# Gates and branch projections of the later layers with tokens on the partitions, the gates' bias added by VectorE

## The reference

```python
h = rmsnorm(x, norm1_g[l])
u = h @ w_in[l]                              # q, k, v, glu_in, four_in
att = ...differential attention of q, k, v, 8 heads, normed
y_a = att @ w_proj_a[l]                      # 512 -> 1024
cv = layernorm(conv31(glu(glu_in)) + conv_b[l], ...)
y_b = jax.nn.silu(cv) @ w_proj_b[l]          # 512 -> 1024
y_c = real(fft2(four_in)) @ w_proj_c[l]      # 512 -> 1024
gates = jax.nn.sigmoid(h @ w_gate[l] + b_gate[l]).reshape(b, s, 3, d)
merged = gates[:, :, 0] * y_a + gates[:, :, 1] * y_b + gates[:, :, 2] * y_c
x = x + merged @ w_out[l]
...then a feed-forward block
```

## Time and profile before

| | us |
|---|---|
| three runs, median (lowest, highest) | 1252.49 (1251.73, 1252.96) |
| the profiled execution | 1253.01 |
| its span | 1251.7 |
| TensorE busy | 1245.6 |
| DVE busy | 948.0 |
| ACT busy | 716.4 |
| POOL busy | 438.8 |

### The profile page before, as it was taken

One profiled execution on the slowest core, in us unless ns is written; L12 is line 12 of the kernel. 1 busy time (PEld: TensorE's weight loads), 2 busy tenths in 40 slices (PEclk: granted clock), 3 DMA queues, 4 the chain that ended last, 5 costly groups with the idle time before them and its releaser, 6 DMA issues.

```text
span 1251.7 us, 18713 instructions
## 1 busy us (share of the span) xinstructions
PE 1245.6 (100%) x7472; PEld 1104.0 (88%) x7472; DVE 948.0 (76%) x1366; ACT 716.4 (57%) x1030; POOL 438.8 (35%) x346
## 2 busy tenths in 40 slices
PE   9999999999999999999999999999999999999999
PEld 7888888888888889999998888888999998888887
DVE  6875668677887478986767888986898586888895
ACT  7755445377765365565846556546456674655552
POOL 0010012039892069467440112008766743011100
PEclk9999999999999999999999999999999999999999
DMA  9753334455545447643455454455753444555443
GB/s 353 254 212 140 135 118 166 171 188 198 189 182 201 169 169 257 210 155 135 169 200 184 175 198 155 182 218 188 265 188 146 156 169 168 196 178 200 151 165 121
DMA packets 36566, 230.73 MB, mean 184 GB/s; under 512 B 4480, under 2 KB 5120, under 8 KB 10496
## 3 DMA queue, kind: packets, MB, share of 16 engines
q1 hardware_dynamic: 36480, 229.55, 51.0%
HBM read 222.19 MB, written 1.05 MB: 178 GB/s over the span
## 4 chain that ended last, share of the span: by engine, by line
PE 97%; DVE 1%; DMA 1%; ACT 1%; SPq 0%; issue 0%; DVEq 0%; ACTq 0%
PE ps L620 19%; PE ps L531 13%; PE ps L533 13%; PE ps L532 13%; PE ps L625 10%; PE ps L586 7%; PE ps L588 7%; PE ps L587 7%; PE ps L536 6%; PE ps L550 2%; DMA raw<-in_w 1%; PE ps L1174 1%; SPq L436 0%; PE ps L851 0%; DVE wlo L1994 0%; ACT whi L1260 0%
## 5 line engine op out<-in xcount | busy, mean ns | idle before, releaser
L1260 ACT ACTIVATE whi<-raw 128x2048 fp32r<-128x2048 f32 (+1 forms) x213 | 401.7, 1891 | 113.2 <-PE ps L533 83.9
L1994 DVE TENSOR_TENSOR wlo<-raw,whi 128x2048 fp32r<-128x2048 f32 (+2 forms) x169 | 383.2, 2273 | 90.1 <-ACT whi L1260 89.4
L1824 POOL TENSOR_TENSOR wlo<-raw,whi 128x512 fp32r<-128x512 f32 x176 | 226.7, 1320 | 90.5 <-ACT whi L1260 87.5
L620 PE MATMUL ps<-hh,whi 128*128 128x512 f32 x1056 | 255.8, 392 | 0.0
L620 PEld LDWEIGHTS ps<-hh,whi 128*128 128x128 f32 x1056 | 193.0, 188 | 36.5
L1796 POOL TENSOR_TENSOR st<-st,sm 128x1 f32<-128x1 f32 (+2 forms) x28 | 46.0, 1643 | 362.5 <-DVE st L2048 193.3
L586 PE MATMUL ps<-hh,whi 128*128 128x256 f32 x512 | 146.2, 285 | 0.0
L588 PE MATMUL ps<-hh,wlo 128*128 128x256 f32 x512 | 144.9, 283 | 0.0
L587 PE MATMUL ps<-hh,whi 128*128 128x256 f32 x512 | 144.8, 283 | 0.0
L625 PEld LDWEIGHTS ps<-hh,wlo 128*128 128x128 f32 x1056 | 137.8, 191 | 6.7
L625 PE MATMUL ps<-hh,wlo 128*128 128x256 f32 x1056 | 139.8, 283 | 0.0
(11 more groups left out here) (348 smaller groups left out, 2252.9 us busy)
## 6 DMA issues: line engine op xcount, KB each, us to landing
raw<-in_w SPq DMA_DIRECT2D x203, 1024.0 KB, 4.8
raw<-in_w SPq DMA_DIRECT2D x8, 256.0 KB, 7.0
kst<-kh SPq DMA_DIRECT2D x16, 128.0 KB, 2.6
qst<-qh SPq DMA_DIRECT2D x16, 128.0 KB, 2.4
raw<-in_w SPq DMA_DIRECT2D x2, 560.0 KB, 14.5
x<-in_x SPq DMA_DIRECT2D x2, 512.0 KB, 5.2
gain<-in_rows SPq DMA_DIRECT2D x2, 512.0 KB, 5.7
kst<-kl SPq DMA_DIRECT2D x8, 128.0 KB, 2.4
```

What stands on the lines that cost most here:

```text
L620: pe.op.matmul(o[:, :], wh[:, k, c], t.hh[:, k, :, :], start=k == 0, stop=False, skip_group_check=True)
L1260: act.op.activation(t.whi[i % NHI][:, c], t.raw[i % NRAW][:, c], ACT.Copy).then_inc(*at("act_hi", ("hi", i)))
L1824: pool.op.tensor_tensor(t.wlo[i % NRAW][:, half(k)], t.raw[i % NRAW][:, half(k)], t.whi[i % NHI][:, half(k)].bitcast(F32), ALU.subtract).t ...
L1994: dve.op.tensor_tensor(t.wlo[i % NRAW][:, c], t.raw[i % NRAW][:, c], t.whi[i % NHI][:, c].bitcast(F32), ALU.subtract).then_inc(*at("dve_lo ...
```

## The change

It is made in both later layers and in four parts.

- The gates and the projections pc, pa and pb are computed by `rows` and no more by `feats`. A gate unit is now 512 columns wide, 6 instead of 12 units per layer, in two chunks of 4 k each; a projection is one chunk as before. `rows_steps` learns units of one chunk. As a step of the back is now 6 matmuls of 512 columns, `weave` takes 2 for 4, and the other counts are about halved.
- The bias of a gate is a row now. SP loads 512 of its values, the same for all partitions, into one half of `gain`, two halves in turn, and DVE adds it as it evacuates the bank; ACT only takes sigmoids, of 128x1024 for a whole unit. Before it loads bias j (j from 2), SP waits for the additions of gate j - 2.
- DVE multiplies with the gate in halves of tokens, POOL adds the first two branches, and DVE adds the third. The mixed result is then turned by TensorE and split from PSUM, by the functions that the first layer uses; the first four turns stand in pb1 after two of its four steps.
- POOL raises two sums to powers before it splits the last chunk of pc, no more after it.

```diff
-        for f in GATES:
-            wide(f"g{l}_{f}", "w_gate_2", l, cols((256 * f, 256)), 8, 8)
+        for n in GATES:
+            wide(f"g{l}_{n}", "w_gate_2", l, cols((512 * n, 512)), 8, 4)
-GATES = (8, 9, 10, 11, 0, 1, 2, 3, 4, 5, 6, 7)
+GATES = (4, 5, 0, 1, 2, 3)
...
 def rows_steps(u):
-    c0, c1 = UNITS[u]
+    chunks = UNITS[u]
+    if len(chunks) == 2:
+        yield "take", chunks[0], 0, 0, 0
+        for k in range(4):
+            for tt in range(2):
+                yield "mul", chunks[0], k, k, tt
+            yield "step", chunks[0], 0, 0, 0
+    i = chunks[-1]
+    yield "take", i, 0, 0, 0
     for tt in range(2):
         for k in range(4):
-            yield "mul", c1, k, 4 + k, tt
+            yield "mul", i, k, 4 * len(chunks) - 4 + k, tt
...
+    def bias(l, j):
+        n = GATES[j]
+        load(f"d_bias{j % 2}", t.gain[:, half(j % 2)],
+             d["in_bias"][l:l + 1, 512 * n:512 * n + 512].to_broadcast([128, 512]), ("gate bias", l, n))
...
+            if i == UNITS[f"v{l}"][0]:
+                sp.wait_ge(*on("xn", ("n3", "n5")[l], 1, 1))
+                bias(l, 0)
+                bias(l, 1)
+            for j in range(2, 6):
+                if i == UNITS[f"g{l}_{GATES[j + 1]}" if j < 5 else f"pc{l}_0"][0]:
+                    sp.wait_ge(*on("gate biased", l, GATES[j - 2]))
+                    bias(l, j)
...
@@ pe_program @@
-            yield 9
+            yield 5
...
-            yield 7
+            yield 4
...
-        back = chain(*[feats(f"g{l}_{f}", *h, 8) for f in GATES],
-                     *[feats(f"pc{l}_{f}", t.frh, t.frl, 4, lambda k: [("fr", l, 3)]) for f in range(2)])
-        weave(chain(fourier(), attention(), after_attention()), back, 4)
+        back = chain(*[rows(f"g{l}_{n}", *h) for n in GATES],
+                     *[rows(f"pc{l}_{f}", t.frh, t.frl, [("fr", l, 3)]) for f in range(2)])
+        weave(chain(fourier(), attention(), after_attention()), back, 2)
...
-        for f in range(2):
-            run(feats(f"pb{l}_{f}", t.cvh, t.cvl, 4, lambda k: [("cv split", l)]))
+        run(rows(f"pb{l}_0", t.cvh, t.cvl, [("cv split", l)]))
+        g = rows(f"pb{l}_1", t.cvh, t.cvl)
+        steps(g, 2)
+        for tt in range(2):
+            mixed_turned(f"out{l}", 0, tt)
+        run(g)
...
@@ pe_program, to_x @@
-        if m:
-            for k in range(4):
-                for tt in range(2):
-                    part(0, [k], tt)
-        else:
-            for tt in range(2):
-                part(0, range(4), tt)
-                mixed_turned(1, tt)
+        for tt in range(2):
+            part(0, range(4), tt)
+            mixed_turned(u, 1, tt)
...
@@ pool_program @@
         split(*UNITS[f"pc{l}_0"])
-        split(*UNITS[f"pc{l}_1"])
         power(("o2 rs", l), st[:, 256:272], st[:, 240:256], ("o2 mean", l))
         power(("cv rstd", l), st[:, 274:276], st[:, 272:274], ("cv mean", l))
+        split(*UNITS[f"pc{l}_1"])
...
@@ dve_program @@
+        def gate_out(n):
+
+            def out(tt):
+                name = (f"g{l}_{n}", tt)
+                dve.wait_ge(*on("got", *name))
+                dve.wait_ge(*on("gate bias", l, n))
+                dve.op.tensor_tensor(t.gm2[:, n, tt, :], bank(name)[:, :], t.gain[:, half(GATES.index(n) % 2)],
+                                     ALU.add).then_inc(
+                    *at("dve_out", ("free", name), *([("gate biased", l, n)] * tt)))
+            return out
...
+                dve.op.tensor_tensor(m if b == 2 else g, bank(name)[:, :], g, ALU.mult).then_inc(
                     *at("dve_out", ("free", name)))
+                if b == 1:
+                    await_own("dve_out")
+                    dve.wait_ge(*on("two merged", l, f, tt))
+                    dve.op.tensor_tensor(m, m, g, ALU.add).then_inc(*at("dve_small", ("merged", f"out{l}", f, tt)))
...
+        run(rows(f"pb{l}_0", branch_out(1, 0)))
+        g = rows(f"pb{l}_1", branch_out(1, 1))
+        steps(g, 1)
+        mixed_lower(f"out{l}", 0)
+        run(g)
+        mixed_lower(f"out{l}", 1)
```

More of the change, by code:

```diff
@@ L551, in turned, with rows @@
         ins.then_inc(*at("pe_turned", name))
-    def rows(u, hi, lo):
-        b = {}
+    def rows(u, hi, lo, data=()):
+        for w in data:
+            pe.wait_ge(*on(*w))
+        b, last = {}, 4 * len(UNITS[u]) - 1
         for what, i, k, kg, tt in rows_steps(u):
@@ L561, in rows @@
                 wh, wl = weights(i, t.whi[i % NHI]), weights(i, t.wlo[i % NRAW])
-                ends = [("got", u, tt)] if kg == 7 else []
+                ends = [("got", u, tt)] if kg == last else []
                 if tt == 1 and k == 3:
@@ L565, in rows @@
                 mul3(t.pb[b[tt]][:, 0:n], hi[:, kg, tok(tt)], lo[:, kg, tok(tt)], wh[:, k, :], wl[:, k, :],
-                     kg == 0, kg == 7, ends)
+                     kg == 0, kg == last, ends)
             elif what == "step":
@@ L1771, in after_attention @@
             upper(("cv hi", l), t.cvh[:, :, :], t.csq[:, :, :], ("cv silu", l))
-        back = chain(*[feats(f"g{l}_{f}", 8, gate_out(f)) for f in GATES],
-                     *[feats(f"pc{l}_{f}", 4) for f in range(2)])
-        weave(chain(fourier(), attention(), after_attention()), back, 4)
+        back = chain(*[rows(f"g{l}_{n}", gate_out(n)) for n in GATES],
+                     *[rows(f"pc{l}_{f}") for f in range(2)])
+        weave(chain(fourier(), attention(), after_attention()), back, 2)
         run(back)
         for f in range(2):
-            run(feats(f"pa{l}_{f}", 4))
-        for f in range(2):
-            run(feats(f"pb{l}_{f}", 4, lambda p: mixed_upper(f"out{l}", 4 * f + 2 * p, 1)))
+            run(rows(f"pa{l}_{f}"))
+        run(rows(f"pb{l}_0"))
+        g = rows(f"pb{l}_1")
+        steps(g, 2)
+        mixed_upper(f"out{l}", 0)
+        run(g)
+        mixed_upper(f"out{l}", 1)
         to_x(f"out{l}", f"n{4 + 2 * l}", [])
@@ L2810, in branch_out @@
-            return out
-        back = chain(*[feats(f"g{l}_{f}", 8) for f in GATES],
-                     *[feats(f"pc{l}_{f}", 4, branch_out(2, f)) for f in range(2)])
-        weave(chain(fourier(), attention(), after_attention()), back, 4)
+                if b == 1:
+                    await_own("dve_out")
+                    dve.wait_ge(*on("two merged", l, f, tt))
+                    dve.op.tensor_tensor(m, m, g, ALU.add).then_inc(*at("dve_small", ("merged", f"out{l}", f, tt)))
+            return out
@@ L2815, in layer @@
+        back = chain(*[rows(f"g{l}_{n}", gate_out(n)) for n in GATES],
+                     *[rows(f"pc{l}_{f}", branch_out(2, f)) for f in range(2)])
+        weave(chain(fourier(), attention(), after_attention()), back, 2)
         run(back)
         for f in range(2):
-            run(feats(f"pa{l}_{f}", 4, branch_out(0, f)))
-        for f in range(2):
-            run(feats(f"pb{l}_{f}", 4, branch_out(1, f)))
-        mixed_lower(f"out{l}", 6, 1)
+            run(rows(f"pa{l}_{f}", branch_out(0, f)))
```

158 lines of the change are left out of this document (68 added, 90 removed).

## The result

| us | before | after |
|---|---|---|
| median of the runs | 1252.24 (1251.56 to 1253.26, 11 runs) | 1257.58 (1253.54 to 1258.95, 11 runs) |
| ratio to before | | 1.0037, 95% interval 1.0029 to 1.0045 |
| profiled execution, its span | 1253.01, 1251.7 | 1255.79, 1254.5 |
| mean granted clock of TensorE | 1.000 | 0.996 to 1.000 |

What follows compares the result with a forecast made beforehand. TensorE was taken to bound the kernel; -11.3 + 3.6 + 1.0 = -6.7 us on the profiled 1253.01 gave 1246.3, as a median 1245.8 us. Range 1244.3 to 1250.3, the forecast's own 1244.8 to 1247.5.

Steps and rivals of the forecast that it cites:

- Part 1: Gates and projections of the later layers: 432 fewer matmuls per layer at 13.1 ns save 11.3 us in the two.
- Rival D: Matmul distances: the fixed 13 ns per matmul do not go; 1257.1, or 1254.9 by the page's 2.5 ns; chance 0.03.
- Part 2: pb1 and output product: 16 added transposes per layer cost TensorE 3.6 us in all, their handoff nothing.
- rival C: Slower, from pb1 on: turning the mixed result is exposed because DVE is late; in full 1260.7; chance 0.04.
- rival B: Attention: SP's wait makes chunk loads late and ACT stands; 1250 to 1252.5, no change; chance 0.07.
- Part 3: Attention: gate evacuation moves from ACT to DVE, whose lateness stays covered before W's reader; 0, bounds 0 and 1.5 us per layer.
- rival A: Attention: DVE becomes the bound, its added gate additions partly uncovered; 1247.8 to 1250.4; chance 0.23.
- The rest, at nothing: Behind attention, POOL's split after the powers has 1.1 us of cover; SP's later loads are in time too; cost 0.
- Part 4: End of attention: TensorE waits for DVE's two convolution sums, 0.5 us per layer, bounds 0 and 1.3.

Runs made afterwards that it cites:

- e1: The changed kernel, but POOL splits the last chunk of pc before it raises the two sums to powers; 1250.20 us, ratio 0.9984 to before.
- e2: The changed kernel, but DVE takes the last gate's two additions before its split of pa's first chunk; 1248.35 us, ratio 0.9970 to before.
- e3: The changed kernel with the edits of e1 and e2 together; 1248.43 us, ratio 0.9967 to before.
- e6: e3 with DVE's two sums of the convolution moved ahead of the fifth gate's second addition; 1246.13 us, ratio 0.9953 to before.
- e5: e2 with DVE doing the addition for the last gate's first token half six times; 1258.64 us, ratio 1.0054 to before.
- e4: e2 with the first of the last gate's two additions ahead of the wait for the power and the copies; 1248.50 us, ratio 0.9971 to before.

## Why the prediction was wrong

**Part 1, the matmuls: right, with a remainder.** 114 matmuls of 512 columns outside attention took 25.97 us, 0.228 each, for 0.2267. In attention twelve take 2.75 us instead of 2.72, their starts 0.23 apart and now and then 0.24, so attention gave 2.39 us per layer instead of 2.99. Why the distance is a little longer there no run tells. Rival D is out. The formula that the prediction takes from the Trainium skill, "TensorE: Matmul & The Clock Gate", section "Back-to-back issue gap", is given there for a single matmul by itself; for a stream with weight loads the section has about 131 ns at 512 columns, still further from the 227 measured here.

```profile
614.48:640.45 25.97, 25.97 (x117) 21.43 (x116) 23.41 (x22) 14.84 (x13) 5.09 (x4) 1.00 0.57 197
```

**Part 2, the transposes: right.** Eight take 0.79 us and the follower's follower comes 0.31 later; four take 0.36. Nothing waits, rival C is out. So is rival B: in the two attention stretches and those behind them ACT waited for a chunk to land for 0.2 and 0.5 us in all, and TensorE never:

```profile
640.45 1.03 PE L566 MATMUL ps<-sm,mg 128*128 128x128 f32 x8
641.24 0.48 PE L547 MATMUL ps<-whi,cvh 128*128 128x512 f32 x1
641.55 0.40 PE L548 MATMUL ps<-wlo,cvh 128*128 128x512 f32 x1
```

**Part 3, cost 0: this step failed.** It asked what DVE's lateness does to W, and there it was right: TensorE waits for no W, and rival A is out. But an evacuation has two who wait for it, the one who reads the result and the one who needs the bank, and the second was not followed to the end of the gates. As long as ACT evacuated, what DVE had in its queue did not matter to a bank. With DVE evacuating, everything between "the last gate is in its bank" and the addition does: the wait for the power, the copies, the split of pa's first chunk. The order could have been read off: in DVE's queue both copies and that split stand between the power and the last gate's additions, and before's rows give their lengths (0.36 and 2.29 us). By these lengths alone the wait would have been small, as e1's first layer shows with 0.45 us; the size came with the next step.

**The rest, at nothing: this one failed as well, and by more.** POOL's split behind the powers was judged only by when TensorE wants it. TensorE did not wait for it, but by less than was worked out: the split took 7.1 us where the prediction had 5.1 to 5.7, and ended 15.9 us behind the product with csq (610.92 to 595.02) where it had 14.6 at the most. What it was moved beside was not asked. The earlier trace rows had the sign: the sums at 1.74 and 1.40 us beside POOL, 0.68 for the first without it. Moving POOL's 7 us beside DVE's copies and split put 3.3 us into the queue in front of the bank. Without that (e1) the wait is 0.45 and 1.65 us, and the other order (e2) leaves 0.15. In the forecast's sum both steps stood at 0; they measured 3.45 us per layer, and in the profiled execution 1.2 us of clock behind one of the waits.

**Part 4, 0.5 us: right in mechanism, smaller here.** In the first layer X is 588.56. The addition began at X + 3.86 (worked out 3.85), POOL's split ended at X + 5.39 (5.4), the first sum was slow and the second quick:

```profile
592.42 0.69 DVE L2809 TENSOR_TENSOR gm<-ps,gain 128x512 f32<-128x512 f32 x1 [2.07 <-PE ps L549]
593.03 1.48 DVE L2756 TENSOR_TENSOR csq<-cv 128x512 f32<-128x512 f32 x1
594.54 0.42 DVE L2758 TENSOR_TENSOR csq<-csq 128x256 f32<-128x256 f32 x1
...
588.91 5.04 POOL L1836 TENSOR_TENSOR wlo<-raw,whi 128x512 fp32r<-128x512 f32 x4
```

The first sum took 1.48 us, not 1.75, and TensorE lost 0.1 us, 0.3 in the second layer. Its upper bound is real: where POOL's next split followed at once, both sums were slow (1.62 and 1.42 us in e1, 1.75 and 1.38 in e3) and TensorE lost 1.2 and 1.3 us in one layer.

Of the DVE instructions beside POOL's split the sums, the chunk's split and the copies are longer; the additions from PSUM are not (0.68 to 0.69 us in every kernel), and neither is the reduction of 128x1024 in SBUF (1.21 us, in e1 beside POOL as elsewhere without it). The Trainium skill, "SBUF — State Buffer", section "SBUF: two separate sides", has it so: a DVE instruction with two SBUF inputs, or one in a 2-port mode such as an fp32 copy within SBUF, and a POOL instruction lock each other out of a shared port for the whole of an instruction. The trace agrees for the copies: each began 0.06 us or less behind the start of one of POOL's pieces and ended 0.08 us behind its end, two of them 2.57 us, two of POOL's pieces 2.55. The prediction cited the page for the sums and for the additions, which don't collide, and not for the copies and the split in front of them, which do.

**The sum.** Forecast 1246.3 for the profiled execution, measured 1255.79, 9.5 more: 6.9 for the two waits, 1.2 for the half clock in one layer, 1.2 for attention's distances, and 0.4 in what is left behind attention (part 4's wait 0.6 smaller than forecast, the rest 1.0 longer), less 0.2 elsewhere. With both waits and part 4's gone (e6), 1246.13 was measured. That this is near the forecast's 1245.8 is in part chance, for the forecast has a wait of 1.0 us in it that e6 has not: without any wait it gave 7.7 us of gain, and e6 has 5.8. So three quarters of the gain of parts 1 and 2 was there all along, and was more than eaten by one bank per layer. None of the four rivals had this mechanism: C, slower with 1260.7, was for another reason.

## What to carry to other kernels

When evacuation moves to another engine, list for every bank who needs it next, and read what stands in the new engine's queue ahead of the instruction that frees it, in the stretches between two phases above all, where long waits and odd work are interleaved. A move in one engine's queue is also a move beside others: price what it will run next to, with the rows in which the two engines meet. And a wait of some microseconds on TensorE may cost more than its length; take its bound with the clock at the lower level behind it.

## What the hardware showed beyond that

- A DVE copy of 128x128 fp32 from a broadcast column takes 0.36 us for two, and 2.57 us for two beside POOL's 128x512 subtraction, a factor of 7; a 128x2048 split goes from 2.29 to 3.38 us. POOL's four 128x512 pieces take 5.01 us beside the copies and additions from PSUM (e5) and 7.07 where DVE's split runs too.
- Which of the two is held up goes by which began first. After the change DVE's split began at 606.40, 0.05 us behind POOL's third piece, and took 3.38; POOL's fourth began at 607.59, inside DVE's split, and took 3.33. In e2 DVE's split began at 607.45, as POOL's third piece ended, and took its usual 2.28; POOL's fourth, at 607.45 too, took 3.43. In e4 the split began 0.65 us behind a piece and took 2.80. POOL's pieces of the last chunk, ns shortest/median/longest, after the change and in e2:

```profile
L1836 POOL TENSOR_TENSOR wlo<-raw,whi x4: 1283/1302/3326, 603.8 to 607.6; 128x512 fp32r<-128x512 f32 x4
L1836 POOL TENSOR_TENSOR wlo<-raw,whi x4: 1288/1294/3429, 603.7 to 607.5; 128x512 fp32r<-128x512 f32 x4
```

- TensorE's clock fell to the 1.2 GHz level behind a single wait of 3.5 us in a stream otherwise busy, by the mean clock in ten executions and not in the eleventh, with the same program. It stayed there for 2.7 us in the one trace of the changed kernel, and in e5 for 3.5 us and, in the second layer, for about 5; there eight turns of 128x128 took 1.56 us instead of 0.79.
